# Dilated queries and keys projected already turned, GpSimd's modulation in 256-column pieces, probabilities divided on ScalarE

## What is computed

```python
for layer in range(2):
    p = rms_norm(x) @ w_in[layer]              # 1024 -> c_q 384, c_kv 256, k_r 32, gate_a 512, dil_qkv 4608, gate_b 512
    a = mla_attention(c_q, c_kv, k_r, ...) * silu(gate_a)       # 8 heads over all 512 keys
    b = dilated_attention(dil_qkv, ...) * silu(gate_b)          # 3 groups x 8 heads of 64
    x = x + concat(a, b) @ w_out[layer]
# dilated attention, per group g (window 128, 512, 2048; stride 1, 4, 16):
q, k = partial_rope(q), partial_rope(k)        # the first 16 of the 64 columns of a head are rotated
s = q @ k.T * 64 ** -0.5, masked to the group's band;  softmax;  @ v
# the three groups are mixed by the softmax of their log-sums
# second block:  m = silu(cond) @ mod_w + mod_b      (mod_w: 1024 x 6144, two layers)
```

## Time and profile before

| | before |
|---|---|
| three runs, us | 2333.35, 2335.18, 2335.68 |
| the profiled execution's own time | 2331.19 us |
| its span | 2329.6 us |
| granted TensorE clock, mean | 0.939 |
| TensorE matmul busy | 2105.8 us (90%) |
| VectorE busy | 880.1 us (38%) |
| GpSimd busy | 613.3 us (26%) |
| ScalarE busy | 524.1 us (22%) |

### The profile page before, as it was taken

How to read it: one execution, slowest core, us unless ns; L and a number is a source line. 1 busy time by engine, 2 the same in 40 slices (tenths; PEclk the granted TensorE clock), 3 DMA queues, 4 the chain that set the end, 5 groups by cost and what they waited for, 6 DMA issues and landing times. The chain is left out here.

```text
span 2329.6 us, 23681 instructions
## 1 busy us (share of the span) xinstructions
PE 2105.8 (90%) x8308; PEld 1194.7 (51%) x8308; DVE 880.1 (38%) x1674; ACT 524.1 (22%) x1213; POOL 613.3 (26%) x443
## 2 busy tenths in 40 slices
PE   7999999999999999999997696996999599787995
PEld 5555566555465556666542354645444244454442
DVE  1564453446214552332424447533232400443223
ACT  3233221214113332221311114510111110101110
POOL 4666666666656640000000021000110100001001
PEclk9999999999999999999998798995999699877998
DMA  7323333443343354111012501016895621063994
GB/s 288 131 86 132 125 136 136 144 154 117 132 150 118 131 195 169 55 55 73 37 73 99 212 1 37 1 59 244 302 367 224 226 72 36 0 250 140 369 368 176
DMA packets 69139, 338.90 MB, mean 145 GB/s; under 512 B 8567, under 2 KB 10165, under 8 KB 55477
## 3 DMA queue, kind: packets, MB, share of 16 engines
q1 hardware_dynamic: 36518, 217.02, 24.8%
q0 software_dynamic: 27920, 103.82, 12.6%
q10 hardware_dynamic: 4608, 16.78, 1.8%
HBM read 292.51 MB, written 45.09 MB: 145 GB/s over the span
## 5 line engine op out<-in xcount | busy, mean ns | idle before, releaser
L355 PE MATMUL psA<-ring,gB 128*128 128x384 f32 (+1 forms) x1792 | 582.7, 483 | 1.2 <-ACT gB L646 1.2
L355 PEld LDWEIGHTS psA<-ring,gB 128*128 128x128 f32 x1792 | 335.5, 190 | 219.2 <-issue 7.8
L302 POOL TENSOR_TENSOR wm<-wm,cs 128x2048 f32<-128x2048 f32 x56 | 202.0, 3606 | 135.0 <-DMA wm<-in_mod_w 134.3
L305 POOL TENSOR_TENSOR wm<-wm 128x1024 f32<-128x1024 f32 x112 | 205.1, 1831 | 40.4 <-issue 32.4
L830 DVE COPY probT<-psT 128x512 f32<-128x512 f32 x96 | 66.2, 690 | 375.0 <-PE psT L344 375.0
L1305 POOL COPY idx<-idx 128x1 int32 (+1 forms) x32 | 5.9, 183 | 714.2 <-DVEq L1898 481.9
L851 DVE TENSOR_SCALAR prob<-prob,rl 128x768 f32<-128x768 f32 (+1 forms) x128 | 138.5, 1082 | 10.3
L666 ACT ACTIVATE xn<-psA 128x256 f32<-128x256 f32 x96 | 36.8, 384 | 428.7 <-PE psA L355 428.7
L1436 PE MATMUL psSO<-wreg,arena 128*128 128x512 f32 x256 | 115.3, 593 | 1.9 <-DVE arena L1920 1.9
L1421 PE MATMUL psA<-wreg,arena 128*128 128x512 f32 x256 | 116.2, 608 | 0.0
L363 PE MATMUL psA<-gB,ring 128*128 128x512 f32 x256 | 114.1, 599 | 0.0
(11 more groups left out here) (277 smaller groups left out, 2812.1 us busy)
## 6 DMA issues: line engine op xcount, KB each, us to landing
wm<-in_mod_w POOLq DMA_DIRECT2D x56, 1024.0 KB, 7.8
ring<-in_w_d SPq DMA_DIRECT2D x24, 1536.0 KB, 6.7
wreg<-in_w_gu SPq DMA_DIRECT2D x16, 2048.0 KB, 8.5
wreg<-in_w_dn SPq DMA_DIRECT2D x32, 1024.0 KB, 12.3
mixT<-in_w_gu SPq DMA_DIRECT2D x8, 2048.0 KB, 8.5
aT<-in_w_gu SPq DMA_DIRECT2D x8, 2048.0 KB, 8.4
ys_scratch<-arena ACTq DMA_DIRECT2D x32, 512.0 KB, 9.8
ys_scratch<-qtab POOLq DMA_DIRECT2D x1, 12288.0 KB, 35.5
```

The lines of the kernel that those rows point to most:

```text
L302: nc.gpsimd.tensor_tensor(wm[:, b], wm[:, b], c_all.to_broadcast([P, KD, MCH]), ALU.mult)
L305: nc.gpsimd.tensor_tensor(wm[:, b, 0:n], wm[:, b, 0:n], wm[:, b, n:2 * n], ALU.add)
L355: m = nc.tensor.matmul(psA[:, n % 2, 0:cols], hT[:, k, tile(t)], w[:, k, :], start=(k == 0), stop=(k == KD - 1))
```

## The change

1. Queries and keys of the dilated groups are projected with `columns`, so they come out with features on the partitions, and `turn_qk` and its copies are gone. Values of all three groups of a head pair are projected together by `tokens` (384 columns, `project_v`). Per head pair that is 6 projections of 512 and 4 of 384 in place of 12 of 384 and six turned blocks of 512. Their places in the steps are new.
2. The rotation now works on features-by-tokens tiles of 128 x 512: VectorE shuffles partitions out of PSUM (`STREAM_SHUFFLE`), multiplies the PSUM bank by a cosine table of 128 x 512 (which frees the bank), copies the turned probabilities of head 0, and only then does the second half: a multiplication by the sine table and an addition, both from SBUF to SBUF.
3. `divided` moves to ScalarE (`activation` Copy with a per-partition scale, in place); VectorE keeps the reciprocal (`inverted`, `rl_ready`).
4. GpSimd's multiplication of 2048 columns becomes eight of 256, the additions of 1024 and 512 become four and two of 256.
5. The 1/8 and its sign go into the masked maximum (`-HD ** -0.5` in place of 1.0, mask times -8). The mask's cast to bf16 goes from step 2 to step 1 of layer 0. Weights are laid out and loaded anew: `w_qk` (1 MB), `w_v` (1.5 MB), `w_gb` in four pieces; the rotation table of the dilated heads grows from 64 KB to 512 KB.

```diff
-            def dilated(L, hp, g, slot):
-                load(slot, d["w_d"][L, hp, g], KD * 384)
+            def queries_keys(L, hp, g):
+                slot, at, loaded, _ = QK_SLOT[hp][g]
+                sp.dma_start(ring[:, slot, at:at + 2048], d["w_qk"][L, hp, g]).then_inc(w_loaded[loaded], 16)
...
-                nc.gpsimd.tensor_tensor(wm[:, b], wm[:, b], c_all.to_broadcast([P, KD, MCH]), ALU.mult)
+                for k in range(KD):
+                    nc.gpsimd.tensor_tensor(wm[:, b, k], wm[:, b, k], c_all[:, k].to_broadcast([P, MCH]), ALU.mult)
                 pool.drain()
                 for n in (4, 2):
-                    nc.gpsimd.tensor_tensor(wm[:, b, 0:n], wm[:, b, 0:n], wm[:, b, n:2 * n], ALU.add)
+                    for k in range(n):
+                        nc.gpsimd.tensor_tensor(wm[:, b, k], wm[:, b, k], wm[:, b, n + k], ALU.add)
                     pool.drain()
...
-            def turn_qk(L, e, hp, g):
-
-                tiles = 4 * L + hp
-                pe.wait_ge(dil_roped, GROUPS * tiles + g + 1)
-                for c in range(2):
-                    turn(TT * L + e + c, [tp[:, TP_ROW[g], t, tile(c)] for t in range(NT)])
+            def project_qk(L, hp, g, c):
+
+                slot, at, loaded, count = QK_SLOT[hp][g]
+                pe.wait_ge(w_loaded[loaded], 16 * (LOADS[loaded] * L + count))
+                w = eighths(slot, at, 2 * P)
+                columns(PA * L + pa_qk(hp, g, c), lambda k: w[:, k, tile(c)], hT, range(KD))
+
+            def project_v(L, hp, t):
+
+                slot, count = (0, 2 + hp) if hp else (2, 1)
+                pe.wait_ge(w_loaded[slot], 16 * (LOADS[slot] * L + count))
+                tokens(PA * L + pa_v(hp, t), t, width(slot, 384), 384)
...
                         if j < 3:
                             if t in (0, 2):
-                                project_d(L, 0, (1, 1, 2)[j], (2 * j + t // 2) % 4)
+                                project_qk(L, 0, j, t // 2)
...
                             if t < 2:
-                                project_d(L, 0, 2, 2 + t)
+                                project_qk(L, 1, 0, t)
                             elif t == 2:
                                 project_ga(L, 3, n + 2)
                             else:
-                                project_d(L, 1, 0, 0)
+                                project_qk(L, 1, 1, 0)
                             mla_turn(L, m, 0)
-                            if t:
-                                turn_qk(L, t_first(t - 1), 0, t - 1)
...
+                        if hp == 3:
+                            project_gb(L, t)
+                        elif t == 3:
+                            project_v(L, hp + 1, 3)
+                        elif hp:
+                            project_qk(L, hp + 1, t, 0)
+                        else:
+                            project_qk(L, 1, (1, 2, 2)[t], (1, 0, 1)[t])
+                        dil_turn(L, hp, t, 0)
                         if hp < 3 and t < 3:
-                            for i in range(2):
-                                if hp or t or i:
-                                    project_d(L, hp + 1, t, i)
-                            dil_turn(L, hp, t, 0)
-                            for i in range(2, 4 if t < 2 else 3):
-                                project_d(L, hp + 1, t, i)
-                        elif hp < 3:
-                            project_d(L, hp + 1, 2, 3)
-                            turn_qk(L, t_next(hp, 0), hp + 1, 0)
-                            dil_turn(L, hp, t, 0)
-                            turn_qk(L, t_next(hp, 1), hp + 1, 1)
-                            turn_qk(L, t_next(hp, 2), hp + 1, 2)
-                        else:
-                            project_gb(L, t)
-                            dil_turn(L, hp, t, 0)
+                            if hp:
+                                project_qk(L, hp + 1, t, 1)
+                            project_v(L, hp + 1, t)
                         dil_turn(L, hp, t, 1)
...
+            def divided(L, m, h, keys):
+                act.wait_ge(rl_ready, 2 * (STEPS * L + m) + h + 1)
+                nc.scalar.activation(prob[:, h, 0:keys], prob[:, h, 0:keys], ACT.Copy, scale=rl[:, h:h + 1]).then_inc(p_normed, 1)
...
+            def queries_keys_out(L, hp, g, c):
+
+                n = PA * L + pa_qk(hp, g, c)
+                out = qk_buf[hp % 2][g][:, c, :]
+                dve.drain()
+                dve.wait_ge(pa_ready, n + 1)
+                nc.vector.stream_shuffle(swapped[:], psA[:, n % 2, :], SWAP)
+                nc.vector.tensor_tensor(out, psA[:, n % 2, :], ropeD[:, 0, :], ALU.mult).then_inc(pa_copied[n % 2], 1)
+
+            def rotated(hp, g, c):
+
+                out = qk_buf[hp % 2][g][:, c, :]
+                dve.drain()
+                nc.vector.tensor_tensor(swapped[:], swapped[:], ropeD[:, 1, :], ALU.mult)
+                dve.drain()
+                nc.vector.tensor_tensor(out, out, swapped[:], ALU.add).then_inc(qk_roped, 1)
...
-            def divided(L, m, h, keys):
+            def inverted(L, m, h):
 
                 dve.wait_ge(p_ready, 2 * (STEPS * L + m) + h + 1)
-                nc.vector.reciprocal(rl[:, h:h + 1], lsum[:, h:h + 1])
-                dve.drain()
-                nc.vector.tensor_scalar(prob[:, h, 0:keys], prob[:, h, 0:keys], rl[:, h:h + 1], None, ALU.mult)\
-                    .then_inc(p_normed, 1)
+                nc.vector.reciprocal(rl[:, h:h + 1], lsum[:, h:h + 1]).then_inc(rl_ready, 1)
```

328 lines of the change are left out of this document (162 added, 166 removed).

## The result

The changed kernel took **2271.82 us** (median of four runs, 2270.55 to 2274.13); the kernel before, on the same chip, 2334.44 (2333.35 to 2335.68). The ratio is 0.9733 (95% interval 0.9716 to 0.9750): 62.6 us faster, where 2283 (2273 to 2301) was forecast. So the sign and the cause were right, and the time fell 1.2 us under the range. The profiled execution took 2271.20 us, 0.6 under the median; its span is 2269.6 and its mean granted clock 0.944.

A forecast was written before the change was run, and what follows sets the result against it. The prediction took TensorE, busy for 90% of the span, as the bound. From 2331.19 us it took 56.0 for turning and waits, added 3.5 for new work (2278.7), then 4.0 from profile to median: 2283 us, range 2273 to 2301.

The forecast's parts named there:

- Projections and turning: TensorE's attention steps in both layers: removing turned blocks and waits saves 56.0 us, 19.47 in layer 1, 36.53 in layer 0.
- The new copies, the division, the loads: New VectorE copies and ScalarE's division mostly hidden under TensorE's work; changed loads cost nothing.
- all that is new: The charge for the new copies, division, cast and loads together: 3.5 us, bounds 0 and 12.
- The 2 us that were put on the short MLA steps of layer 0: Rotation's second half waits for GpSimd pieces ahead of the maximum: about 2 us over three pairs.
- the up to 1 us of the cast: The mask's cast, one step earlier and ahead of two copies that free banks: up to 1 us once.
- From the profile to the median: Whole kernel: the median of runs lies 4.0 us above the profiled execution's time, so 2278.7 becomes 2283 us.
- The second block: The part after the two attention layers: the forecast's sum has no term for it.
- A: GpSimd keeps the ports through its queued pieces, delaying VectorE in layer 0: 8 to 18 us, chance 0.10.
- B: GpSimd becomes the bound, pausing 0.36 us per added piece: about 2433 us; chance 0.05 beyond its threshold.
- C: VectorE's copy of the turned head is late in both layers: 8 to 15 us, 2288 to 2298; chance 0.13.
- D: Turning on TensorE was hidden anyway, so removing it gains nothing; chance 0.01, shared with other causes of no difference.

The follow-up runs named there:

- e12: The changed kernel unaltered, run and profiled a second time: 2273.12 us.
- e8: The kernel before unaltered, run and profiled a second time: 2333.15 us.
- e18: The kernel before unaltered, run and profiled a third time: 2334.89 us.
- e1: The kernel before with only GpSimd's multiplication cut into eight pieces: 2315.40 us, ratio 0.9919 to before.
- e2: The kernel before with only the division moved from VectorE to ScalarE: 2317.76 us, ratio 0.9928 to before.
- e6: The kernel before with both GpSimd's pieces and the division on ScalarE: 2317.07 us, ratio 0.9925 to before.
- e9: The kernel before with GpSimd's arithmetic left out except the last addition of 256 columns: 2334.94 us, ratio 1.0004 to before.
- e7: The changed kernel with the rotation's second half ahead of the copy of the turned head: 2290.79 us, ratio 0.9816 to before.
- e5: The changed kernel with GpSimd's instructions whole and the division on VectorE again: 2291.52 us, ratio 0.9820 to before.
- e20: The changed kernel with a drain behind every GpSimd piece, eleven more a load: 2285.24 us, ratio 0.9786 to before.
- e3: The changed kernel with only GpSimd's instructions made whole again: 2279.71 us, ratio 0.9757 to before.

## Why the prediction was right, and where it was wrong

The time is 11.2 us under the forecast, and the step lengths are not the reason: three other terms of the sum were mis-sized, by 3.5, 3.4 and 4.0 us.

**Projections and turning.** Right, and the mechanism with it. The sum was -19.47 for layer 1 and -36.53 for layer 0; between the first profiles they are -19.38 (432.34 - 451.72) and -36.64 (582.29 - 618.93). In layer 1 every term holds to 0.1 us. In layer 0 the agreement is partly luck: the MLA pairs grew by 10.10 us where 9.75 was forecast, and the stretch behind the three dilated pairs shrank by 0.48, which was forecast as nothing. Steps priced from differences of other steps carried over, although the order was new.

**The new copies, the division, the loads.** "I charge 3.5 us for all that is new" is the first step that failed: it measured about 0 in two profiles and 2.0 in the third (e12). The shuffle stayed under the scores, as its value of 0.69 said, and the division cost nothing. The 2 us that were put on the short MLA steps of layer 0 did not occur, nor did the up to 1 us of the cast: layer 0's MLA pairs take 169.86 us, layer 1's, which have no cast, 169.85. From 30 to 1111 us the granted clock is 1.00, as the prediction asked.

**From the profile to the median.** "The median of the runs is 4.0 us above it, so I predict 2283 us" is the second step that failed. It carries an offset of one profile of the old kernel over to the new one; the changed kernel's profile stands 0.6 under its median, so this is 3.4 of the 11.2 us, beside the 3.5 above and the 4.0 below (0.3 is rounding). Why the offset shrank is shown only in part. The first profile of before had the cheapest layer 0 of three, by 4.6 and 7.1 us, and the change takes GpSimd's interference away. But e8, with 7.1 us more in layer 0, took only 2.0 us more in all, since its second block was 4.1 shorter.

**The second block** was put at nothing, and this is the third and largest term. Its code is unchanged, but the first profile of before spent 1031.32 us in it and that of after 1027.31: the other 4.0 us. The window rows of the two:

```profile
1298.23:2329.55 1031.32, 877.35 (x3034) 475.34 (x3034) 361.71 (x798) 180.89 (x435) 76.96 (x100) 0.88 0.45 172
```

```profile
1242.26:2269.57 1027.31, 874.36 (x3034) 474.09 (x3034) 361.72 (x798) 181.19 (x435) 77.03 (x100) 0.89 0.46 173
```

Same matmuls, same VectorE time, 3.0 us less on TensorE at a clock of 0.89 for 0.88. Over the profiles of all kernels with the reference's modulation the block takes 1026.71 to 1033.51, so I take the 4.0 for chance; no run isolates it. One order there is: the six profiles with the old layout (before, e8, e18, e1, e2, e6) spread over 6.8 us, the nine with the new one over 1.8 (1027.31 to 1029.13). The runs point the same way: the four or five of each new-layout kernel lie within 2.0 to 4.8 us, those of e1, e2 and e6 within 7.5 to 8.9 and e9's ten within 8.9, though the first four of before lie within 2.3. So the spread seems to go with the layout and not with GpSimd's arithmetic, which e9 leaves out; why is open. By the means of three profiles each, layer 0 brings 39.9 us, layer 1 19.2, the second block 1.6 and the start 0.9: 61.6 us, where the medians are 62.6 apart.

**Rivals.** A: not the usual course, but its mechanism exists: five holds of about 5 us in eight profiles, at most 2.0 us of time in one execution, where 8 to 18 were priced. B: kept off by the missing drains; its price per pause was right to 0.01 us, its cost to TensorE too high. C: absent, and e7 shows that the order of the copies keeps it absent. (Its 8 to 15 us on 2283 would have been 2291 to 2298, not 2288 to 2298.) D: refuted by the steps, and by e5, where the turned projections alone bring 1.8%.

## What to carry to other kernels

Where an engine is busy all the time, price a change from differences between its own steps: here each term was right to 0.5 us, and the sum of 56 to 0.1. Shared ports make the price of an engine's instruction depend on the length of the other's: cut the long ones, but leave out the drains, and move what is held away from the path. An offset between one profile and the median belongs to its kernel; if the change removes a cause of it, take several profiles, or leave the offset out.

## What had not been expected of the hardware

- Two queued GpSimd instructions without a drain mostly let VectorE in between (0.94 to 1.17 us for an operation of 0.69), and now and then eight in a row don't (4.74 to 5.37 us, five times in eight profiles).
- A drain behind a GpSimd multiplication of 256 columns cost 0.364 us each (e20).
- After TensorE waits of 2.29 us (e8), 2.50 (e3) and 4.31 (the first profile of before) a stretch at or near half clock follows: a granted clock of 0.57 over 4.0 us, of 0.60 over 4.0 (788 to 792) and of 0.51 over 6.9. Of the 17.06 us that layer 0's dilated pairs took more than layer 1's, 6.65 are longer busy time of TensorE (254.82 against 248.17), the rest waits. A wait of 1.22 us (e12) left the clock at 1.00.
